# Attention's kind C steps dealt out singly between those of kinds A and B

## The reference, cut to what matters

```python
# kind A: 4 heads, 64 wide, dilated windows + distance bias      -> 2 pairs of heads
# kind B: 8 heads, 96 wide, plain softmax attention              -> 4 pairs
# kind C: 4 heads, each with TWO softmaxes of 32-wide queries    -> 2 pairs
def diff_attention(q, k, v, pos, slopes, lam):
    ...
        sc = jnp.einsum('bhcqe,bhcke->bhcqk', qi, k).astype(jnp.float32) * scale
        dist = jnp.abs(pi[:, :, None] - pos[:, None, :]).astype(jnp.float32)
        sc = sc - slopes[None, :, None, None, None] * dist[:, None, None]
        a = jax.nn.softmax(sc, axis=-1)
        return jnp.einsum('bhqk,bhkv->bhqv', a[:, :, 0] - lam * a[:, :, 1], vf)
...
    out_c = rmsnorm_2(o_c, diff_head_norm) * (1.0 - lam_init)
    mixed = jnp.concatenate([out_a..., out_b..., out_c...], axis=-1)
    return mixed @ w_out
```

## Time and profile before

| | us |
|---|---|
| median of 3 runs (lowest to highest) | 3520.54 (3520.06 to 3521.14) |
| the profiled execution's own time | 3522.4 |
| its span | 3519.1 |
| PE busy | 3300.4 (94%) |
| attention of layer 0, from S(0) to out2 | 1708.4 to 1868.0 |
| attention of layer 1 | 2878.6 to 3038.6 |
| granted TensorE clock, mean over the span | 0.973 |

### The profile page before, as it was taken

How to read it: one execution, slowest core, us unless ns; L and a number is a source line. 1 busy time by engine, 2 the same in 40 slices (tenths; PEclk the granted TensorE clock), 3 DMA queues, 4 the chain that set the end, 5 groups by cost and what they waited for, 6 DMA issues and landing times.

```text
span 3519.1 us, 33762 instructions
## 1 busy us (share of the span) xinstructions
PE 3300.4 (94%) x13452; PEld 2430.7 (69%) x13452; DVE 1788.7 (51%) x2979; ACT 491.4 (14%) x990; POOL 86.3 (2%) x102
## 2 busy tenths in 40 slices
PE   5999997589999999999889999999999988999997
PEld 2444444258888888886444888888888834478886
DVE  4025213546633876455373666356653726466643
ACT  1110001110000100010451000010000135310000
POOL 0000000000000000000300000000000130000000
PEclk9989998799999999999999999999999999999998
DMA  4213330012222222221301222222222230022221
GB/s 193 90 48 132 132 143 24 12 60 86 95 84 84 87 84 85 86 93 56 114 1 48 86 94 81 87 87 93 84 87 91 75 120 1 25 84 88 92 82 50
DMA packets 41836, 285.50 MB, mean 81 GB/s; under 512 B 5104, under 2 KB 5104, under 8 KB 10704
## 3 DMA queue, kind: packets, MB, share of 16 engines
q1 hardware_dynamic: 37584, 268.71, 21.5%
q0 software_dynamic: 4096, 14.64, 1.3%
HBM read 279.14 MB, written 2.10 MB: 80 GB/s over the span
## 4 chain that ended last, share of the span: by engine, by line
PE 88%; DVE 7%; ACT 2%; DVEq 1%; issue 1%; DMA 1%; POOL 0%; ACTq 0%; POOLq 0%
PE ps L770 59%; PE ps L424 15%; PE ps L443 5%; PE ps L972 2%; PE ps L940 1%; PE ps L706 1%; PE ps L954 1%; ACT arena L1222 1%; DVE arena L1867 1%; PE ps L693 1%; PE ps L716 0%; DMA h<-in_x 0%; PE ps L979 0%; DVE arena L1283 0%; PE ps L911 0%
## 5 line engine op out<-in xcount | busy, mean ns | idle before, releaser
L770 PE MATMUL ps<-arena 128*128 128x256 f32 x4624 | 1056.9, 379 | 0.0
L770 PEld LDWEIGHTS ps<-arena 128*128 128x128 f32 x4624 | 878.6, 190 | 119.5
L770 PE MATMUL ps<-arena,ring 128*128 128x256 f32 x2384 | 555.2, 379 | 0.0
L770 PEld LDWEIGHTS ps<-arena,ring 128*128 128x128 f32 x2384 | 453.0, 190 | 61.6
L770 PE MATMUL ps<-xn,ring 128*128 128x256 f32 x1888 | 436.5, 382 | 15.9 <-ACT xn L1096 6.9
L770 PEld LDWEIGHTS ps<-xn,ring 128*128 128x128 f32 x1888 | 360.7, 191 | 75.6 <-ACT xn L1096 8.5
L424 PE MATMUL ps<-xn,ring 128*128 128x512 f32 x768 | 335.1, 599 | 0.0
L1543 DVE TENSOR_TENSOR arena<-arena,ps 128x512 f32<-128x512 f32 x138 | 94.8, 687 | 421.5 <-PE ps L770 419.5
L1520 DVE TENSOR_TENSOR arena<-ring 128x512 f32<-128x512 f32 x182 | 122.9, 675 | 351.8 <-PE ps L770 351.5
L424 PEld LDWEIGHTS ps<-xn,ring 128*128 128x128 f32 x768 | 147.4, 192 | 186.7 <-issue 186.7
L770 PE MATMUL ps<-xn,arena 128*128 128x256 f32 x1072 | 257.6, 381 | 0.0
(11 more groups left out here) (283 smaller groups left out, 2365.9 us busy)
## 6 DMA issues: line engine op xcount, KB each, us to landing
ring<-in_w_up_a SPq DMA_DIRECT2D x44, 1024.0 KB, 4.8
ring<-in_w_up_b SPq DMA_DIRECT2D x44, 1024.0 KB, 4.8
ring<-in_w_ff SPq DMA_DIRECT2D x32, 1024.0 KB, 4.7
ring<-in_w_ada SPq DMA_DIRECT2D x24, 1024.0 KB, 6.3
ring<-in_w_down_a SPq DMA_DIRECT2D x16, 1024.0 KB, 4.8
ring<-in_w_down_b SPq DMA_DIRECT2D x16, 1024.0 KB, 4.8
ring<-in_w_in SPq DMA_DIRECT2D x14, 1024.0 KB, 4.8
ring<-in_w_out SPq DMA_DIRECT2D x12, 1024.0 KB, 4.8
```

Of the source, the lines that this page charges most:

```text
L770: mm = nc.tensor.matmul(out_ap, w, operand(product, quads[i]), start=at not in opened, stop=last_chunk and i == len(quads) - 1, skip_group ...
```

## The change

The list of groups is replaced by a list of single steps. `PLAIN_STEPS` are the 24 steps of A and B in order; `C_STEPS` the 16 of C. The new order is two A steps, then C and plain by turns until C is used up, then the last plain steps: C stands at n = 2, 4, ..., 32, A at 0, 1, 3, 5, ..., 13, B at 15, 17, ..., 33 and 34 to 39. Since a C pair and an A or B pair are now in flight at once, sums (`sums_p`, `inv_p`) get four places instead of two, and turned weights of C pairs a place of their own (`TURNED_PLACE` 2), which the last B pair uses too. Pairs end at other steps: before at 3, 7, 11, 19, 23, 31, 35, 39, now at 5, 13, 16 (C), 21, 29, 32 (C), 35, 39. GpSimd's wait for window n names the step that A step n-3 has now.

```diff
-ATT_GROUPS = [("A", 0), ("A", 1), ("B", 0), ("C", 0), ("C", 1), ("B", 1), ("C", 2), ("C", 3), ("B", 2), ("B", 3)]
-ATT_STEPS = ST * len(ATT_GROUPS)
+PLAIN_STEPS = [(kind, g, i) for kind, n in (("A", 2), ("B", 4)) for g in range(n) for i in range(ST)]
+C_STEPS = [("C", g, i) for g in range(C_HEADS) for i in range(ST)]
+STEPS = (PLAIN_STEPS[:2] + [x for k, c in enumerate(C_STEPS) for x in (c, PLAIN_STEPS[k + 2])]
+         + PLAIN_STEPS[len(C_STEPS) + 2:])
+ATT_STEPS = len(STEPS)
+A_STEPS = [n for n, x in enumerate(STEPS) if x[0] == "A"]
...
-PAIRS = [g for g in ATT_GROUPS if g in MIX_TILE]
+def pair_key(n):
+    kind, g, _ = STEPS[n]
+    return kind, (g | 1 if kind == "C" else g)
+LAST_STEP = {pair_key(n): n for n in range(ATT_STEPS)}
+PAIRS = sorted(LAST_STEP, key=LAST_STEP.get)
+
+SUM_PLACE = [2 + g // 2 if kind == "C" else (g if kind == "A" else g + 2) % 2 for kind, g in PAIRS]
+TURNED_PLACE = [2 if kind == "C" or (kind, g) == ("B", 3) else 0 for kind, g in PAIRS]
...
-        sums_p = sb("sums_p", [P, 2, 2, ST])
-        inv_p = sb("inv_p", [P, 2, 2, ST])
+        sums_p = sb("sums_p", [P, 4, 2, ST])
+        inv_p = sb("inv_p", [P, 4, 2, ST])
...
-                    pool.wait_ge(sem("minima"), UNITS_2 * layer + 2 * (n - 3) + 2)
+                    pool.wait_ge(sem("minima"), UNITS_2 * layer + 2 * A_STEPS[n - 3] + 2)
...
-                            mm = nc.tensor.matmul(ps[64 * u:64 * u + 64, 6 + j % 2, :], v, probs_t[2 * (j % 2) + u][:, kt, :],
+                            mm = nc.tensor.matmul(ps[64 * u:64 * u + 64, 6 + j % 2, :], v, probs_t[TURNED_PLACE[j] + u][:, kt, :],
...
-                                                  inv_p[:, j % 2, u, i:i + 1].to_broadcast([P, 64]), ident,
+                                                  inv_p[:, SUM_PLACE[j], u, i:i + 1].to_broadcast([P, 64]), ident,
...
-                    dst = probs_t[2 * (pair_of(n) % 2) + (g % 2 if kind == "C" else 0)][:, :, i * P:(i + 1) * P]
+                    dst = probs_t[TURNED_PLACE[pair_of(n)] + (g % 2 if kind == "C" else 0)][:, :, i * P:(i + 1) * P]
...
-                            dve.wait_ge(sem("biases"), 2 * ST * layer + n + 1)
+                            dve.wait_ge(sem("biases"), 2 * ST * layer + A_STEPS.index(n) + 1)
```

More of the change, by code:

```diff
@@ L184, in step @@
 def step(n):
-    kind, g = ATT_GROUPS[n // ST]
-    return kind, g, n % ST
+    return STEPS[n]
 def pair_ending(n):
-    if 0 <= n < ATT_STEPS and n % ST == ST - 1 and ATT_GROUPS[n // ST] in MIX_TILE:
-        return PAIRS.index(ATT_GROUPS[n // ST])
+    if 0 <= n < ATT_STEPS and LAST_STEP[pair_key(n)] == n:
+        return PAIRS.index(pair_key(n))
     return None
 def pair_of(n):
-    return sum(1 for m in range(n) if pair_ending(m) is not None)
+    return PAIRS.index(pair_key(n))
 def turn_uses():
@@ L1218, in exps @@
                         if kind == "C":
-                            total = sums_p[:, j % 2, g % 2, i:i + 1] if u == 0 else other[:, g % 2, 0, i:i + 1]
+                            total = sums_p[:, SUM_PLACE[j], g % 2, i:i + 1] if u == 0 else other[:, g % 2, 0, i:i + 1]
                         else:
-                            total = sums_p[:, j % 2, u, i:i + 1]
+                            total = sums_p[:, SUM_PLACE[j], u, i:i + 1]
                         nc.scalar.activation(dst, ps[:, 2 * (n % 2) + u, :] if kind == "B" else dst, ACT.Exp,
@@ L1862, in least @@
                         if kind == "A":
-                            dve.wait_ge(sem("biases"), 2 * ST * layer + n + 1)
-                            last = nc.vector.tensor_tensor_reduce(prob(unit), src, bias_a(n)[:, u, :],
+                            dve.wait_ge(sem("biases"), 2 * ST * layer + A_STEPS.index(n) + 1)
+                            last = nc.vector.tensor_tensor_reduce(prob(unit), src, bias_a(A_STEPS.index(n))[:, u, :],
                                                                   SLOPES[2 * (2 * g + u)], 3.0e38, ALU.add, ALU.min, out_min)
@@ L1876, in join @@
                     dve.wait_ge(sem("exps"), UNITS_2 * layer + 2 * n + 2)
-                    one = sums_p[:, pair_of(n) % 2, g % 2, i:i + 1]
+                    one = sums_p[:, SUM_PLACE[pair_of(n)], g % 2, i:i + 1]
                     total, inv, by = (other[:, g % 2, x, i:i + 1] for x in range(3))
@@ L1887, in invert @@
                     dve.wait_ge(sem("exps"), UNITS_2 * layer + 2 * n + 2)
-                    nc.vector.reciprocal(inv_p[:, j % 2, :, :], sums_p[:, j % 2, :, :]).then_inc(sem("inverted"), 1)
+                    nc.vector.reciprocal(inv_p[:, SUM_PLACE[j], :, :], sums_p[:, SUM_PLACE[j], :, :]).then_inc(sem("inverted"), 1)
                 def turned(n):
@@ L1894, in turned @@
                     dve.wait_ge(sem("turned5"), TURNS[1] * layer + TURN["turn", n, 1] + 1)
-                    dst = probs_t[2 * (pair_of(n) % 2) + (g % 2 if kind == "C" else 1)][:, :, i * P:(i + 1) * P]
+                    dst = probs_t[TURNED_PLACE[pair_of(n)] + (g % 2 if kind == "C" else 1)][:, :, i * P:(i + 1) * P]
                     nc.vector.tensor_copy(dst, ps[:, 5, :].rearrange("p (t s) -> p t s", t=ST)).then_inc(sem("copied5"), 1)
```

## The result

| | before | after |
|---|---|---|
| median of 5 runs (lowest, highest), us | 3521.14 (3520.06, 3522.27) | 3535.08 (3533.18, 3541.58) |
| profiled execution / its span, us | 3522.4 / 3519.1 | 3533.18 / 3531.4 |
| attention, layer 0 / layer 1, us | 159.5 / 160.0 | 164.9 / 165.3 |

The ratio is 1.0043 with an interval of 1.0028 to 1.0058: the change makes the kernel slower by 14 us, where 12 us less was forecast, and the time lies outside the range of 3497 to 3523. The span grew by 12.3 us: 5.4 and 5.3 in the two attention stretches, and 1.7 between them. There the changed order does nothing, and a kernel with the old order and small additions (experiment 3) shows the same 1.7; I come back to it at the end. Within the attention the way from S(0) to S(39) is only 0.4 us longer than before in either layer, and the tail from S(39) to out2 is 5.0 longer.

A forecast was written before the change was run, and what follows sets the result against it. Waits between engines were taken to set the attention's pace. Per layer: A and C steps -6.3, rest to step 39 -4.3, tail +2.4, slow clock +2.2, sum -6.0; both layers -12, giving 3508.5 us, range 3497 to 3523.

The forecast's parts named there:

- rival 3: Late bias additions on GpSimd and joins on DVE hinder each other: 3516 or 3532, lower bound 0; priced 0, chance 0.04.
- held for the whole addition: Upper case of GpSimd additions against joins: each addition holds one join throughout, 23.6 us over both layers, time 3532.
- Front, S(0) to S(14): From the scores of step 0 to those of step 14, A and C steps alternating: forecast 34.4 us.
- The gap of 5.06 us: PE's wait at the attention's start for the first late bias: forecast to be gone.
- the W costs 3.3 in the A stretch: Weigh at step 9 stands in an A step's wait and swallows 1.2 us of idle time, costing 3.3 instead of 4.46.
- Middle: Scores of step 14 to step 39: B and C loops of 5.62 us; 97.5 us with one slow weigh.
- the head: Head sums at step 23: the inverse on DVE delays the weigh at 25 by 5.6 us; one slow weigh adds 2.2.
- The slow W forecast for step 25: One weigh at lowered clock behind PE's 3.1 us gap at the head sums: +2.2 us per layer, bounds 0 and 15.
- Tail: Scores of step 39 to out2: head sums stand behind a weigh, 21.6 us against 19.2 before, +2.4.
- Rival 1: Loops longer than their rows, a C turn waiting for a copy: 15 loops 0.4 us longer, 3520.5; chance 0.20.
- Rival 2: Lower clock takes over among alternating A and C steps: +9 us per layer, 3538; chance 0.12.
- Rival 4: All waits hide and PE becomes the bound, B and C loops 4.4 instead of 5.62 us: 3479; chance 0.08.

The follow-up runs named there:

- experiment 3: Kernel before, old order, with GpSimd's five late bias additions per layer touching one column per head: 3518.00 us, ratio 0.9987.
- experiment 2: Changed kernel with each late bias addition cut into eight pieces of 64 columns per head, all computed: 3523.15 us, ratio 1.0006.
- experiment 1: Changed kernel with the late bias additions touching one column per head instead of 512: 3521.35 us, ratio 0.9998.
- experiment 4: Kernel before with extra useless GpSimd additions, multiplications and memsets beside C steps (steps 13 and 26): 3533.3 us in one run.
- experiment 5: Changed kernel with head sums issued ahead of the weigh on PE where both fall in one step (step 39 only): 3528.65 us, ratio 1.0019.
- experiment 7: Changed order with C one step earlier (1, 3, ... 31) and the bias additions in eight pieces: 3523.24 us, ratio 1.0006.

## Why the prediction was wrong

**The step that failed** is the price in rival 3: "I take 0, since the reductions beside additions kept their 0.69 us". The reductions read PSUM and one SBUF tile, joins read two SBUF tiles, and the row bore on the first sort only. It still holds after the change (0.68 at 1718.57). "No row shows such an overlap" was wrong as well: it was true of the attention, but 20 us ahead of it the trace of the kernel before has the pair. There GpSimd adds the distances to the first three windows, and DVE multiplies two SBUF tiles:

```profile
1682.93 6.96 POOL L588 TENSOR_TENSOR xn<-xn,arena 128x1024 f32<-128x1024 f32 x3 [4.59 <-DMA xn<-in_log_c]
```

```profile
1688.55 1.89 DVE L1799 TENSOR_TENSOR xn<-xn,arena 128x512 f32<-128x512 f32 x1
...
1721.66 0.20 DVE L1888 RECIPROCAL inv_p<-sums_p 128x8 f32<-128x8 f32 x1
...
2864.72 0.68 DVE L1799 TENSOR_TENSOR xn<-xn,arena 128x512 f32<-128x512 f32 x1
```

Alone, at 2864.72, this multiplication takes 0.68; beside the last of GpSimd's three, which ends at 1689.89, it takes 1.89 and ends 0.55 behind it. The reciprocal at 1721.66, with one SBUF input, runs beside a late addition and keeps its 0.20. These rows would have priced the join at the whole addition.

After the change three of the five additions per layer hold a DVE instruction, each until the addition ends, 7.3 and 7.1 us of DVE, and some 12 to 14 us of the kernel's time (experiments 2 and 1; the tiny additions of experiment 1 are also done sooner, but no A reduction of the changed kernel waits for one). Experiment 4 shows the hold outside this order, and experiment 2 that cutting the additions lifts most of it. The case "held for the whole addition", 3532, stood in the text at a chance of 4 in 100 with both prices; it is the mechanism that happened, with three of five additions instead of all. That its 3532 lies near the measured time is luck: it had 23.6 us of holds against a gain of 12, and there were 14.4 against a gain of next to nothing. The rule of the Trainium skill's page "GPSIMD Engine Reference" (section "1. Specifications"), that contention with GpSimd comes with VectorE instructions that have two SBUF inputs, was right against the row that I set against it: such joins took up to 3.35 instead of 0.75 us.

**Front, S(0) to S(14).** The gap of 5.06 us is gone, as said: in experiment 1, S(5) starts 9.3 us after S(0) and A scores follow every 5.0 us. That the W costs 3.3 in the A stretch was wrong, it costs 4.2, because the turn ahead of it waits for ACT's copy. The loop behind it costs another 0.6, and the slow A scores S(13) with the slow turn behind them 1.3 (S(14) starts 2.94 us after S(13), where S(8) starts 1.65 after S(7)). Together these make 37.0 instead of 34.4. Then the holds make 44.6: 7.6 more, of which 7.3 are the excess of the held instructions, which leaves little for the low clock in the front.

**Middle.** Right: loops of 5.61, and 96.1 us with everything against 95.3 + 2.2. At the head S(23) to S(26) took 19.4, against 12.8 from S(15) to S(18), which also hold one W: 6.6, where 5.6 and up to 2.2 for the clock were counted. The slow W forecast for step 25 came in layer 1 only (5.35 us); in layer 0 it kept its 3.65, and a turn of 1.97 and scores of 2.53 before it were slow instead.

**Tail.** The order of events was right and its length was mis-sized by the clock: 24.2 instead of 21.6, so a term of the sum failed here too. I had priced one slow W per layer, at the head in step 23, and not the gap that the head inverse leaves in the tail too, where 2.99 us of idle PE were followed by a turn of 2.17 and a weigh of 6.27 (+2.6 for the weigh alone). Experiment 5 moves the weigh into the gap and the tail is 20.5.

**The ledger without holds** would be: front -3.7, middle -1.6 and -2.4 (98.0 and 97.2 in experiment 1 against 99.6), tail +4.2 and +4.9, in sum -1.1 in layer 0 and, against a layer 1 of before that is 0.4 longer, -1.7 in layer 1, and 1.7 between the layers against it. That is experiment 1: no difference from before. Of the 6 us per layer forecast 4 to 5 were never there; the other 6.5 and 7.0 of the miss are the holds. The holds are thus about half of the miss, and without them the forecast would still have named a gain that did not come.

**Rival 1** fell: no loop was longer than its rows, but for the one with W. **Rival 2** named 3538, near the measured time, and its sign was there too, a clock of 0.85 in the front. But it is a result here, not the cause: without holds the clock is 0.95 over the attention (experiment 1), and over the first 38 us of layer 0 it is 0.95 in experiment 1, with one slow A scores, and 1.00 in experiment 2. What the low clock costs the changed kernel shows in the tail and between the layers. **Rival 4** fell: PE's work never became what the loops wait for.

## What to carry to other kernels

Before work of one engine is moved beside another's, look up which operands each reads, and not only whether the places and semaphores are free: a row with other operands (here PSUM instead of SBUF) says nothing of the price. Search the whole trace for a pair with the same operands, outside the stretch that changes too; here it stood 20 us ahead. A cost that no row shows deserves its upper bound in the forecast. A gap is best filled with steps that use nothing of what made the gap: here B steps, without joins, gained 5.5 us where C steps lost 14. And an idle stretch of PE of some 3 us that a new order leaves wants a price of its own for what runs behind it (here 2.6 us for one weigh), as a bound and not as a certainty: the last point below has the same gap once with a cost of 1.7 us and once with none.

## What the runs showed of the hardware

- A DVE instruction with two SBUF inputs that comes beside a two-input GpSimd addition lasts until that addition ends, whatever its own size: 0.22 became 2.33 with one element per partition, 0.75 became 3.35 with 512. One with a single SBUF input (a reciprocal, 0.20) or with one input in PSUM (reductions, copies, 0.68) is not held. The addition itself mostly stays near its length (2.34 to 2.37). The hold also goes the other way: the addition that began while a join ran took 2.53, and pieces of 0.45 beside a join took 0.83 to 0.90. Between three long additions DVE got in, one instruction each time (2.28, then 2.86); through short pieces in a row it waited up to 5.18.
- Which of two that start together wins is not settled. At 1717.30 a join began 0.43 us ahead of an addition and kept its 0.75; at 1723.69 one began 0.43 ahead and was held, and in experiment 5 so was the one that answers to 1717.30. Each time GpSimd issued a DMA just before. The profile's spans on GpSimd are rough, so the true order of the starts may be another.
- The same late addition in eight pieces takes 3.3 to 3.8 instead of 2.35 us; joins beside it take 0.83 to 1.16, and the small operation up to 2.75 (experiment 7).
- One-input multiplications on GpSimd held one small operation (0.99) and no join; memsets held nothing; a one-input reciprocal on DVE beside the multiplications kept its 3.35 us. These were seen once each.
- Between the layers, out2 of layer 0 to S(0) of layer 1, the kernel before takes 1010.6 us, and so does experiment 4; all others take 1012.2 to 1012.9, experiment 3 among them, though nothing in that stretch differs. The difference lies in one place: PE idles 2.64 us before and 2.63 after the change, and the matmuls behind that gap run at full clock in the kernel before and at first at half clock in the changed one. These are the 5 us behind the gap, before and then after:

```profile
2818.12:2823.12 5.00, 5.00 (x12) 2.37 (x13) 1.29 (x2) 0.00 (x0) 0.00 (x0) 1.00 0.10 42
```

```profile
2823.43:2828.43 5.00, 5.00 (x8) 2.22 (x9) 1.29 (x2) 0.00 (x0) 0.00 (x0) 0.66 0.10 42
```

  Four passes fewer fit in, at 0.43 us each, which is the 1.7. Why the clock falls behind this gap in one kernel and not in the other stays open.
